# Expert rows added to the outputs by accumulating scatters, the third weight piece fetched during routing, and bias products on four row groups, in a hybrid attention and mixture-of-experts step

## The chip, the cores and the metric

The kernel runs on one core of a Trainium2 chip. The metric is device time in microseconds from start to end of one execution. Engines: TensorE (PE) multiplies matrices and writes PSUM; VectorE (DVE), ScalarE (ACT) and GpSimd (POOL) work element by element; SyncE (SP) issues DMAs. Sixteen DMA engines move data between HBM and SBUF. DMAs that SP or ACT issue go by hardware queues; those that POOL issues, all indirect ones, go by a software queue (q0 in the profile).

## The reference, cut to what matters

One layer for 512 prompt tokens and 8 x 4 sample tokens (544 in all, D = 1024). After three attention-like branches the residual x is complete, and the mixture of experts is added:

```
x = x + mixed @ w_out
logits = h @ router_w + router_b              # h = rmsnorm(x), 32 experts
top, eidx = top_k(logits, 4); gates = softmax(top)
gu   = rows @ w_gu[e] + b_gu[e]               # rows of h, sorted into blocks of one expert
gate = min(gu[:, :1024], 7); up = clip(gu[:, 1024:], -7, 7)
act  = gate * sigmoid(1.702 * gate) * (up + 1)
y    = act @ w_down[e] + b_down[e]
out  = x + sum over the 4 choices of gates * y
```

The outputs that the change touches are y_prompt (512 x 1024) and y_sample (32 x 1024), both float32.

## The kernel before

The program is a row of phases, each an `nc.Block` with one instruction stream per engine and a barrier at its end. Two phases matter here; everything before them (projections, pooling, attention; until about 735 us) is the same in both kernels.

**The routing phase** multiplies the branches by their gates, adds the residual, normalises, computes router logits and sorts the 2176 (token, choice) pairs into blocks of `SLOTS` = 96 rows of one expert. VectorE computes block and slot number of each pair (`blk_f`, `slot_f`), and builds one-hot matrices from them for each tile of 128 tokens (`hot_slot`, `hot_blk`); TensorE multiplies them (L2580) into a table of which token stands in which slot of which block. `spread` (L2587) turns the table so that each partition holds the row numbers that it will gather. `slot_from` is the number of a row's quarter in `scr_h` (normalised x in HBM), `slot_row` that with the choice as well, `slot_gate` the gate. In the same phase the bias b_down is weighted with the gates: `gmat` (token x expert gates) is turned into `gmT` (L2568), and ten products `gmT` x `b_down` (five tiles, two halves of 512) go to PSUM banks (`BD_BANK`); four stand in routing (L2573), six in the next phase (L2888), and VectorE adds all ten to x in the next phase (L2792).

The experts' weights stream through a ring of three slots of 4 MB: two pieces of w_gu, one of w_down, 12 MB a block. The first block's pieces 0 and 1 are issued by SP in the routing phase (L2248, L2253), piece 2 at the start of the next phase (L2662).

**The expert phase** runs a loop over the blocks in use, 32 here. A block's 96 rows are three groups (`G` = 3) of 32 rows, a row cut into four quarters of 256, so that a group is a tile of 128 partitions x 256. Per block:

- POOL copies the index column of block b+1 (L2710) and issues three gathers from `scr_h` into `xg` (L2714); copies gates and target rows of block b (L2729, L2730); for each group waits for ScalarE's scaled result `y_rows` and scatters it into `y_of`, a scratch of 4 x 1024 rows in HBM, one place for each choice of each token (L2735); then it waits until all three scatters have landed (L2739).
- VectorE turns `xg` into `xgT` (L2781) for the next block, and computes the clamped gate between the products.
- TensorE multiplies `xgT` with both w_gu pieces (L2851), then the activation with w_down (L2877), group by group, with the next block's gate bias between (L2861). It waits for `xgT` (e_xT) and for each piece (e_in).
- SP issues each next piece when TensorE has used the slot (L2678).

Indices past the end of the target are dropped (`bounds_check`): that is how padding slots are handled. After the loop SP reads the four rows of each token back from `y_of` (L2687 to L2693), VectorE adds them to x (L2833, L2841), and SP stores the sums as the outputs (L2699, L2702). `x` stays in SBUF throughout.

The order of each engine's instructions is the order in which they are written; nothing is rescheduled.

Of the kernel before, what the change touches and what calls it, by code (L numbers as in the profile page):

```python
# [17 lines left out]
U32 = mybir.dt.uint32  # L18
ALU = mybir.AluOpType
# [194 lines left out]
def build_program(nc, i, o, stop_after=99):  # L214

    ctx = ExitStack()
    with ctx:
# [1898 lines left out]
        slot_row = take(NBLK + 1, GROUPS_E, dt=U32)  # L2116
# [5 lines left out]
        hot_gate = take(NT, TOPK, NE)  # L2122
        assert cursor[0] <= 53000
# [36 lines left out]
        hot_slot = take(2, TOPK, SLOTS)  # L2160
        hot_blk = take(2, TOPK, 2, NBLK + 1)
# [11 lines left out]
        gmT = take(NTOK)  # L2173
# [3 lines left out]
        y_of = scratch("y_of", [TOPK, 1024, D])  # L2177
        hT_at = oT_at - 120 - KD * NTOK
        ring_at = [hT_at, tail_base + KD * D, tail_base]
        end_at = [hT_at, hT_at + 4096, w_gb_at, tail_base + KD * D, tail_base + KD * D + 4096]  # L2180
# [24 lines left out]
        BD_BANK = (1, 2, 3, 4, 5, 6, 7, 0, 1, 2)  # L2205
# [20 lines left out]
        two = lambda ap: ap.rearrange("p (h n) -> p h n", h=2)  # L2226

        with nc.Block() as block:
            @block.sync
            def _(sp):  # L2230
                sp.dma_start(w_up, i["w_up"].rearrange("(k p) n -> p k n", p=128)).then_inc(g_wu, 16)
                for u in range(6, 24):
# [43 lines left out]
            def _(act):  # L2276
# [17 lines left out]
                for n, (cols_n, b) in enumerate(((512, 2), (NTOK - 512, 3))):  # L2294
                    act.wait_ge(r_gmt, n + 1)
                    act.activation(gmT[0:32, 512 * n:512 * n + cols_n], bank(b)[0:32, 0:cols_n], ACT.Copy).then_inc(r_gme, 1)

            @block.vector
            def _(dve):
# [53 lines left out]
                dve.wait_ge(g_rc, 112)  # L2353
# [86 lines left out]
                for n in range(NT):  # L2440
                    r, s = ROWS[n], n % 2
                    if n >= 2:
                        dve.wait_ge(r_hu, n - 1)
                    wide = lambda ap, w: ap.unsqueeze(2).to_broadcast([r, TOPK, w])
                    link(dve.tensor_tensor(hot_blk[0:r, s, :, 1], iota128[0:r, 0:NBLK + 1].unsqueeze(1).to_broadcast([r, TOPK, NBLK + 1]),
                                           wide(blk_f[0:r, n], NBLK + 1), ALU.is_equal))
                    dve.tensor_tensor(hot_slot[0:r, s], iota128[0:r, 0:SLOTS].unsqueeze(1).to_broadcast([r, TOPK, SLOTS]),
                                      wide(slot_f[0:r, n], SLOTS), ALU.is_equal)
                    link(dve.tensor_tensor(hot_blk[0:r, s, :, 0], hot_blk[0:r, s, :, 1], wide(token1[0:r, n], NBLK + 1), ALU.mult))
                    dve.tensor_tensor(hot_blk[0:r, s, :, 1], hot_blk[0:r, s, :, 1], wide(g4[0:r, n], NBLK + 1), ALU.mult  # L2450
                                      ).then_inc(r_hs, 1)
# [4 lines left out]
                dve.wait_ge(r_hu, NT)  # L2456
# [5 lines left out]

                dve.wait_ge(r_sq, 1)
                wide_rows = bank(0)[:, 0:GROUPS_E * 2 * (NBLK + 1)].rearrange("p (g v b) -> p v b g", g=GROUPS_E, v=2)
                dve.tensor_copy(slot_gate, wide_rows[:, 1])
                link(dve.tensor_scalar(slot_row, wide_rows[:, 0], 4.0, cols[:, 4:5], ALU.mult, ALU.add))
                dve.tensor_scalar(slot_from, slot_row, 4095, None, ALU.bitwise_and)

            @block.tensor
            def _(pe):  # L2470
# [21 lines left out]
                pe.wait_ge(g_rc, 112)  # L2492
# [72 lines left out]
                for n in range(NT):  # L2565
                    r = ROWS[n]
                    out = bank(2)[0:32, 128 * n:128 * n + r] if n < 4 else bank(3)[0:32, 0:r]
                    mm = pe.transpose(out, gmat[0:r, n], ident[0:r, 0:r])  # L2568
                    if n >= 3:
                        mm.then_inc(r_gmt, 1)  # L2570
                pe.wait_ge(r_gme, 2)
                for u in range(4):
                    pe.matmul(bank(BD_BANK[u]), gmT[0:32, 128 * (u // 2):128 * (u // 2) + 128],  # L2573
                              b_down[0:32, 512 * (u % 2):512 * (u % 2) + 512], start=True, stop=True).then_inc(p_bd, 1)

                for n in range(NT):
                    r = ROWS[n]
                    pe.wait_ge(r_hs, n + 1)
                    for k in range(TOPK):
                        mm = pe.matmul(bank(7)[0:SLOTS, 128:130 + 2 * NBLK], hot_slot[0:r, n % 2, k],  # L2580
                                       hot_blk[0:r, n % 2, k].rearrange("p v b -> p (v b)"),
                                       start=(n == k == 0), stop=(n == NT - 1 and k == TOPK - 1))
                    mm.then_inc(r_hu, 1)

                pe.wait_ge(r_sp, 1)
                for g in range(GROUPS_E):
                    mm = pe.matmul(bank(0)[:, 2 * (NBLK + 1) * g:2 * (NBLK + 1) * (g + 1)], spread[0:SLOTS, g],  # L2587
# [6 lines left out]
        row_from, row_to = take(4, dt=U32), take(4, dt=U32)  # L2594
# [30 lines left out]
        p_be = sem("p_be")  # L2625
        y_lo = [sem(f"y_lo{n}") for n in range(NT)]
# [316 lines left out]
```

## Time and profile before

| | us |
|---|---|
| median of 3 runs | 1891.73 |
| lowest, highest | 1889.73, 1892.1 |
| span of the profiled execution | 1895.2 |
| TensorE busy | 1738.0 (92%) |
| VectorE busy | 545.6 (29%) |
| ScalarE busy | 335.8 (18%) |
| GpSimd busy | 453.4 (24%) |
| all DMA, mean | 283 GB/s |

The profiled execution is known by its span, from the first instruction to the last; no separate device time is recorded for it. Its span is 3.5 us above the median of the runs. The first 855.7 us of it are everything before the expert blocks, the next 1003 us the 32 blocks, the last 36 us the sums and stores.

### The profile page before, as it was taken

What the parts mean: (1) busy time and instruction counts of PE and PEld (TensorE: products, weight loads), DVE (VectorE), ACT (ScalarE), POOL (GpSimd) and SP (SyncE); (2) the same over time, 40 slices, a digit from 0 to 9 for tenths busy, and PEclk for the clock granted to TensorE, in tenths of its full rate; (3) what the DMA queues carried; (4) which work ended last, traced back from release to release, by engine and by line L of the source; (5) the groups of instructions that cost most, each with busy time, mean ns of one, the idle gap of its engine ahead of it and who ended that gap; (6) DMA issues with size and microseconds to landing.
All of it is one profiled execution on the core that took longest, in us unless ns stands there. A gap on an engine that the chain in (4) does not pass through costs nothing.

```text
span 1895.2 us, 40017 instructions
## 1 busy us (share of the span) xinstructions
PE 1738.0 (92%) x16117; PEld 1000.8 (53%) x16117; DVE 545.6 (29%) x1355; ACT 335.8 (18%) x736; POOL 453.4 (24%) x522
## 2 busy tenths in 40 slices
PE   7997886688899999969999999999999999999992
PEld 3545773344588886533445673555563445443441
DVE  2222014266111111362323131313232323222225
ACT  3232222265200000001111111111111111111110
POOL 1113537376100003311212222222212122222220
PEclk9997977798899999969999999999999999999996
DMA  8207867440421103146999999999999999999986
GB/s 303 100 31 236 301 188 245 160 158 1 178 79 56 56 22 117 45 185 270 416 426 420 422 416 420 420 424 422 415 423 408 422 423 419 423 420 409 426 356 243
DMA packets 84034, 535.54 MB, mean 283 GB/s; under 512 B 19552, under 2 KB 43584, under 8 KB 71009
## 3 DMA queue, kind: packets, MB, share of 16 engines
q1 hardware_dynamic: 62921, 493.44, 64.6%
q0 software_dynamic: 14544, 32.03, 5.0%
q10 hardware_dynamic: 6512, 9.33, 1.5%
q8 instruction: 33, 0.54, 0.1%
q14 instruction: 24, 0.20, 0.0%
HBM read 518.32 MB, written 28.39 MB: 288 GB/s over the span
## 4 chain that ended last, share of the span: by engine, by line
PE 53%; DMA 2%; DVE 0%; SPq 0%; issue 0%; POOLq 0%; POOL 0%; ACT 0%
PE psum L2851 35%; PE psum L2877 18%; DMA arena<-y_of 1%; DMA arena<-scr_h,arena 1%; PE psum L2861 0%; DVE arena L2841 0%; SPq L2689 0%; DMA y_of<-arena 0%; SPq L2687 0%; DVE arena L2781 0%; POOLq L2648 0%; POOL arena L2718 0%; ACT arena L2767 0%; POOLq L2722 0%; POOLq L2718 0%
## 5 line engine op out<-in xcount | busy, mean ns | idle before, releaser
L2851 PE MATMUL psum<-arena 128*32 128x512 f32 x6144 | 668.9, 592 | 3.8 <-DVE arena L2781 2.2
L2851 PEld LDWEIGHTS psum<-arena 128*32 128x32 f32 x6144 | 249.0, 108 | 404.0 <-issue 401.1
L2877 PE MATMUL psum<-arena 128*32 128x256 f32 x6144 | 345.4, 378 | 0.0
L2877 PEld LDWEIGHTS psum<-arena 128*32 128x32 f32 x6144 | 252.0, 109 | 94.0 <-issue 9.8
L2806 DVE TENSOR_TENSOR arena<-psum,arena 128x512 f32<-128x512 f32 x96 | 66.4, 692 | 573.9 <-PE psum L2851 573.9
L2735 POOL DMA_INDIRECT y_of<-arena x96 | 96.9, 1009 | 473.0 <-ACT arena L2767 473.0
L2480 PE MATMUL psum<-arena 128*128 128x272 f32 x768 | 182.9, 396 | 1.8 <-PEq L231 1.8
L2480 PEld LDWEIGHTS psum<-arena 128*128 128x128 f32 x768 | 146.7, 191 | 35.5 <-issue 3.4
L2763 ACT ACTIVATE arena<-arena 128x256 f32<-128x256 f32 x96 | 40.1, 418 | 611.7 <-DVE arena L2808 611.7
L2714 POOL DMA_INDIRECT arena<-scr_h,arena x96 | 99.0, 1031 | 49.3 <-POOL arena L2710 28.5
L799 PE MATMUL psum<-arena 128*128 128x512 f32 (+1 forms) x256 | 90.7, 513 | 0.2 <-DVE arena L660 0.2
L2767 ACT ACTIVATE arena<-psum,arena 128x256 f32<-128x256 f32 x96 | 45.6, 475 | 245.7 <-PE psum L2877 245.7
L2307 DVE TENSOR_TENSOR arena<-psum,arena 128x544 f32<-128x544 f32 x24 | 17.4, 725 | 218.5 <-ACT arena L2282 218.5
L1883 POOL TENSOR_SCALAR arena<-arena 128x512 f32<-128x512 f32 (+3 forms) x64 | 68.5, 1082 | 26.7 <-DVE arena L2010 26.5
L2710 POOL COPY arena<-arena 128x3 uint32 x32 | 6.0, 188 | 279.7 <-DMA y_of<-arena 232.4
L1213 PE MATMUL psum<-arena 128*128 128x256 f32 x256 | 66.0, 415 | 5.5 <-issue 5.5
L2781 DVE STREAM_TRANSPOSE arena<-arena 128x768 f32<-128x768 f32 x33 | 32.2, 977 | 129.5 <-DMA arena<-scr_h,arena 129.5
L422 POOL CAST arena<-arena 32x8 bf16<-32x8 f32 (+1 forms) x6 | 6.2, 1032 | 263.8 <-DMA arena<-in_b_gu 256.9
L799 PEld LDWEIGHTS psum<-arena 128*128 128x128 f32 x256 | 44.1, 191 | 46.9 <-issue 46.6
L444 POOL DMA_INDIRECT arena<-in_cache_slc,arena x60 | 56.9, 949 | 49.0 <-POOLq L231 23.6
L2487 PE MATMUL psum<-arena 128*128 128x272 f32 x256 | 64.3, 399 | 2.3 <-DMA arena<-in_w_up 2.3
L1213 PEld LDWEIGHTS psum<-arena 128*128 128x128 f32 x256 | 52.4, 209 | 15.2 <-issue 5.9
(365 smaller groups left out, 1485.7 us busy)
## 6 DMA issues: line engine op xcount, KB each, us to landing
arena<-in_w_gu SPq DMA_DIRECT2D x64, 4096.0 KB, 15.0
arena<-in_w_down SPq DMA_DIRECT2D x32, 4096.0 KB
arena<-in_w_gb SPq DMA_DIRECT2D x24, 512.0 KB, 3.5
arena<-y_of SPq DMA_DIRECT2D x8, 1024.0 KB, 15.1
arena<-in_cache_cmp SPq DMA_DIRECT2D x62, 128.0 KB, 4.3
arena<-in_cache_slc SPq DMA_DIRECT2D x60, 128.0 KB, 3.0
arena<-in_w_tok SPq DMA_DIRECT2D x3, 2048.0 KB, 12.8
arena<-in_x_all SPq DMA_DIRECT2D x8, 512.0 KB, 11.0
```

The costliest lines, as they stand in the source:

```text
L444: pool.indirect_dma_start(dst, None, i[table], bass.IndirectOffsetOnAxis(page_row[:, at:at + 1], 0)).then_inc(sem, 16)
L799: mm = pe.matmul(bank(2 + c)[0:r, 0:b - a], dstT(n)[:, k], w_tok[:, k, a:b], start=(k == 0), stop=(k == KD - 1))
L1213: mm = pe.matmul(sum_bank(s, c)[:, 0:2 * n].rearrange("p (g b m) -> p g b m", g=2, b=PAGES), w_cmp[:, c, j], turned, start=(j == 0), stop= ...
L1883: ins = pool.tensor_scalar(rows, rows, c[:, g:g + 1], None, ALU.mult)
L2480: pe.matmul(bank(4 * s + h)[:, 0:HALF], w_gb[:, u % 6, k], hT[:, k, t], start=(k == 0), stop=(k == KD - 1))
L2487: mm = pe.matmul(bank(4 * s + 2 + h)[:, 0:HALF], w_up[:, k, 128 * c:128 * c + 128], oT_of(k)[:, t], start=(k == k0), stop=(k == k1 - 1))
L2714: pool.indirect_dma_start(xg[:, g], None, h_quarters, bass.IndirectOffsetOnAxis(row_from[:, g:g + 1], 0), bounds_check=4 * NTOK - 1, oob_i ...
L2735: pool.indirect_dma_start(y_quarters, bass.IndirectOffsetOnAxis(row_to[:, g:g + 1], 0), y_rows[:, g], None, bounds_check=4 * 1024 * TOPK - ...
L2767: act.activation(y_rows[:, g], dn_half(g), ACT.Copy, scale=cur_gate[:, g:g + 1]).then_inc(e_yc, 1)
L2806: dve.tensor_tensor(gu_c[:, g], gu_bank(g), bias_sb, ALU.add).then_inc(e_ba, 1)
L2851: mm = pe.matmul(gu_bank(g)[32 * j:32 * j + 32].rearrange("p (h n) -> p h n", h=2), xgT[:, g, 32 * k:32 * k + 32], gu_w(slot)[:, part, :, ...
L2877: mm = pe.matmul(dn_half(g)[32 * j:32 * j + 32], actT[:, g, 32 * k:32 * k + 32], dn_w(slot)[:, part, 256 * j:256 * j + 256], start=(k == 0 ...
```

## The change

1. The scratch `y_of` and the sums at the end are gone. When the ten bias products are added to x, SP writes x itself to y_prompt and y_sample (five stores, semaphore p_out). POOL waits for them, and then in each block and for each group issues two scatters that add to their target (`compute_op=ALU.add`) instead of one that stores: one into y_prompt by `slot_from`, which drops sample rows, and one into y_sample by `slot_smp` (`slot_from` with the bit of 2048 flipped), which drops prompt rows. POOL waits for all six before it goes on.
2. The third weight piece of block 0 is issued at the end of the routing phase.
3. The bias products: `gmT` and `b_down` stand four times on groups of 32 partitions, so that products of different tiles lie on different row groups of TensorE; order, banks and places are new. Six stand in routing, two of the additions too.
4. The one-hot matrices are built in three batches into buffers of their own instead of two that are reused.

On POOL, in the expert loop, from the gathers of the next block to the loop's end. Before (names: `scr_h` the rows to gather, `y_of` the scratch, `arena` SBUF):

```order
L2714 DMA arena<-scr_h,arena 128x256 x3
L2729 ISA
L2729 COPY arena<-arena 128x3
L2730 ISA
L2730 COPY arena<-arena 128x3
L2731 ISA
L2733 REGISTER_ALU
L2735 DMA y_of<-arena 16384x256
L2733 REGISTER_ALU
L2735 DMA y_of<-arena 16384x256
L2733 REGISTER_ALU
L2735 DMA y_of<-arena 16384x256
```

The same place after the change, from the third copy on:

```order
L2732 COPY arena<-arena 128x3
L2733 REGISTER_ALU
L2735 REGISTER_ALU
L2737 DMA out_y_prompt<-arena 2048x256
L2740 DMA out_y_sample<-arena 128x256
L2735 REGISTER_ALU
L2737 DMA out_y_prompt<-arena 2048x256
L2740 DMA out_y_sample<-arena 128x256
L2735 REGISTER_ALU
L2737 DMA out_y_prompt<-arena 2048x256
L2740 DMA out_y_sample<-arena 128x256
```

One scatter for each group has become two, and a third index copy stands ahead of them.

On TensorE, the end of routing and the start of the expert phase, from the turning of `gmat` to the first block's gate bias. Before:

```order
L2568 MATMUL psum<-arena 32x128 x4
L2568 MATMUL psum<-arena 32x32
L2573 MATMUL psum<-arena 128x512 x4
L2580 MATMUL psum<-arena 96x110 x20
L2587 MATMUL psum<-arena 128x110 x3
```
```order
L2888 MATMUL psum<-arena 128x512 x4
L2888 MATMUL psum<-arena 32x512 x2
L2893 MATMUL psum<-arena 32x512 x4
```

And after, where L2244 is the bias product:

```order
L2593 MATMUL psum<-arena 32x128 x4
L2593 MATMUL psum<-arena 32x32
L2244 MATMUL psum<-arena 128x512 x4
L2606 MATMUL psum<-arena 96x110 x8
L2244 MATMUL psum<-arena 128x512 x2
L2606 MATMUL psum<-arena 96x110 x12
L2616 MATMUL psum<-arena 128x110 x3
```
```order
L2244 MATMUL psum<-arena 128x512 x2
L2244 MATMUL psum<-arena 32x512 x2
L2873 MATMUL psum<-arena 32x512 x4
```

Two bias products moved from the expert phase into routing, between the one-hot products of the first two tiles and the rest.

The diff, cut to its core:

```diff
@@ routing
-        hot_slot = take(2, TOPK, SLOTS)
-        hot_blk = take(2, TOPK, 2, NBLK + 1)
+        hot_slot = take(NT * TOPK, SLOTS)
+        hot_blk = arena[:, w_gb_at:w_gb_at + NT * TOPK * 2 * (NBLK + 1)].rearrange("p (k v b) -> p k v b", v=2, b=NBLK + 1)
-        BD_BANK = (1, 2, 3, 4, 5, 6, 7, 0, 1, 2)
+        BD_UNIT = [(n, h) for h in range(2) for n in range(NT - 1)] + [(NT - 1, 0), (NT - 1, 1)]
+        BD_BANK = (1, 2, 3, 4, 5, 0, 1, 2, 3, 4)
+        BD_EARLY = 6
+        HOT_BATCHES = ((0, 2), (2, 4), (4, NT))
+        def bias_added(dve, u):
+            n, h = BD_UNIT[u]
+            r = ROWS[n]
+            dve.wait_ge(p_bd, u + 1)
+            sl = x[0:r, n, 512 * h:512 * h + 512]
+            dve.tensor_tensor(sl, bank(BD_BANK[u])[0:r], sl, ALU.add).then_inc(p_be, 1)
+        def bias_product(pe, u):
+            n, h = BD_UNIT[u]
+            r, q = ROWS[n], 32 * (n % 4)
+            at = 128 if n == NT - 1 else 0
+            pe.matmul(bank(BD_BANK[u])[0:r], gmT[q:q + 32, at:at + r], b_down[q:q + 32, 512 * h:512 * h + 512],
+                      start=True, stop=True, tile_position=(q, 0)).then_inc(p_bd, 1)
@@ routing, SP
-                                         (b_down[0:32], i["b_down"]),
+                                         *((b_down[32 * q:32 * q + 32], i["b_down"]) for q in range(4)),
+                sp.wait_ge(x_rt, NT)
+                sp.wait_ge(x_lg, NT)
+                sp.wait_ge(r_bp, 12)
                 sp.wait_ge(x_st[0], 48)
                 sp.wait_ge(x_st[1], 32)
+                sp.dma_start(ring[2], weights(slice(0, 1), 2)).then_inc(e_in[2], 16)
@@ routing, VectorE
+                bias_added(dve, 0)
-                dve.wait_ge(r_hu, NT)
+                dve.wait_ge(r_hu, len(HOT_BATCHES))
...
+                bias_added(dve, 1)
                 dve.wait_ge(r_sq, 1)
...
-                dve.tensor_scalar(slot_from, slot_row, 4095, None, ALU.bitwise_and)
+                link(dve.tensor_scalar(slot_from, slot_row, 4095, None, ALU.bitwise_and))
+                dve.tensor_scalar(slot_smp, slot_from, 4 * NP_TOK, None, ALU.bitwise_xor)
@@ expert phase, SP
-                sp.dma_start(ring[2], weights(slice(0, 1), 2)).then_inc(e_in[2], 16)
+                sp.wait_ge(p_be, 2 * NT)
+                for n in range(NT):
+                    sp.dma_start(out_p[128 * n:128 * n + 128] if n < NT - 1 else out_s, x[0:ROWS[n], n]).then_inc(p_out, 16)
...
-                for g in range(G):
-                    sp.wait_ge(e_out[g], blocks * 16)
-                (the ten read-backs from y_of and the six stores)
@@ expert phase, POOL
                 pool.sem_inc(e_sent, 1)
+                pool.wait_ge(p_out, 16 * NT)
...
-                                    pool.indirect_dma_start(y_quarters, bass.IndirectOffsetOnAxis(row_to[:, g:g + 1], 0),
-                                                            y_rows[:, g], None, bounds_check=4 * 1024 * TOPK - 1, oob_is_err=False
-                                                            ).then_inc(e_out[g], 16)
+                                    pool.indirect_dma_start(p_quarters, bass.IndirectOffsetOnAxis(row_to[:, g:g + 1], 0),
+                                                            y_rows[:, g], None, bounds_check=4 * NP_TOK - 1, oob_is_err=False,
+                                                            compute_op=ALU.add).then_inc(e_out[g], 16)
+                                    pool.indirect_dma_start(s_quarters, bass.IndirectOffsetOnAxis(row_smp[:, g:g + 1], 0),
+                                                            y_rows[:, g], None, bounds_check=4 * NS * TS - 1, oob_is_err=False,
+                                                            compute_op=ALU.add).then_inc(e_out[g], 16)
                                 for g in range(G):
-                                    pool.wait_ge(e_out[g], 16 * b + 16)
+                                    pool.wait_ge(e_out[g], 32 * b + 32)
@@ expert phase, VectorE
-                (the sums over the four choices)
```

## Rows read from the trace of the kernel before

**Rows 1.** The page: the span, and the software DMA queue (packets, MB, share).
```profile
span 1895.2 us, 40017 instructions
...
q0 software_dynamic: 14544, 32.03, 5.0%
```

**Rows 2.** The chain that ended last: start us, us, what; one block, then the end.
```profile
1639.75 20.60 PE psum L2851 x192
...
1670.93 20.60 PE psum L2851 x192
...
1860.20 2.36 DMA y_of<-arena
...
1868.47 18.41 DMA arena<-y_of
```

**Rows 3.** Stretches (busy by engine, granted clock, DMA share, GB/s); SP's last weight piece.
```profile
1257.70:1288.90 31.20, 31.20 (x394) 18.16 (x390) 8.59 (x20) 4.43 (x9) 6.61 (x9) 1.00 1.00 420
1840.00:1842.00 2.00, 2.00 (x24) 0.62 (x19) 0.57 (x1) 0.00 (x0) 1.69 (x2) 1.00 0.13 49
...
1827.82 0.33 SPq L2678 DMA_DIRECT2D arena<-in_w_down  x1
```

**Rows 4.** Timeline of POOL and VectorE in that block: start, us, instruction, [idle before <-releaser].
```profile
1634.02 1.04 POOL L2735 DMA_INDIRECT y_of<-arena  x1 [9.82 <-ACT arena L2767]
1641.12 0.98 POOL L2735 DMA_INDIRECT y_of<-arena  x1 [2.43 <-ACT arena L2767]
1650.61 0.19 POOL L2710 COPY arena<-arena 128x3 uint32 x1 [8.50 <-DMA y_of<-arena]
1651.68 1.06 POOL L2714 DMA_INDIRECT arena<-scr_h,arena  x1 [0.89 <-POOL arena L2710]
1654.37 1.04 POOL L2714 DMA_INDIRECT arena<-scr_h,arena  x1 [0.30 <-issue]
1668.35 0.98 DVE L2781 STREAM_TRANSPOSE arena<-arena 128x768 f32<-128x768 f32 x1 [5.33 <-DMA arena<-scr_h,arena]
```

**Rows 5.** Waits from 900 to 1855 us: total, times, longest.
```profile
POOL arena L2710 <- DMA y_of<-arena: 232.4, 27, 9.2
DVE arena L2781 <- DMA arena<-scr_h,arena: 127.6, 30, 5.7
```

**Rows 6.** Timeline around the first block.
```profile
841.32 10.71 PE L2888 MATMUL psum<-arena 32*128 32x512 f32 x12 [2.06 <-PEq L231]
844.74 1.00 POOL L2718 DMA_INDIRECT arena<-scr_h,arena  x1 [0.30 <-issue]
852.07 0.68 DVE L2792 TENSOR_TENSOR arena<-psum,arena 32x512 f32<-32x512 f32 x1 [1.03 <-PE psum L2888]
855.70 1.93 PE L2851 MATMUL psum<-arena 128*32 128x512 f32 x8 [2.19 <-DVE arena L2781]
855.76 0.19 POOL L2710 COPY arena<-arena 128x3 uint32 x1 [10.02 <-DVE arena L2781]
```

**Rows 7.** Timeline in routing.
```profile
822.73 7.19 PE L2573 MATMUL psum<-arena 32*128 32x512 f32 x8 [0.59 <-ACT arena L2296]
829.84 3.17 PE L2580 MATMUL psum<-arena 128*96 128x110 f32 x16
831.66 0.39 DVE L2445 TENSOR_TENSOR arena<-arena 128x220 f32<-128x220 f32 x1 [3.48 <-PE psum L2580]
```

**Rows 8.** DMA issues: count, KB each, median us from issue to landing.
```profile
arena<-in_w_gu SPq DMA_DIRECT2D x64, 4096.0 KB, 15.0
arena<-scr_h,arena POOLq DMA_INDIRECT x99, 10.6
y_of<-arena POOLq DMA_INDIRECT x96, 8.1
arena<-in_cache_slc,arena POOLq DMA_INDIRECT x60, 4.2
arena<-in_cache_cmp,arena POOLq DMA_INDIRECT x48, 5.6
```

More of the change, by code:

```diff
@@ L2122, in build_program @@
         hot_gate = take(NT, TOPK, NE)
+        slot_row = take(NBLK + 1, GROUPS_E, dt=U32)
         assert cursor[0] <= 53000
@@ L2172, in build_program @@
         gmat = take(NT, NE)
-        gmT = take(NTOK)
+        gmT = take(128 + 32)
         b_down = take(D)
@@ L2565, in _ @@
                 for n in range(NT):
[L2566 to L2570, printed above, removed]
+                    r, q = ROWS[n], 32 * (n % 4)
+                    at = 128 if n == NT - 1 else 0
+                    mm = pe.matmul(bank(0)[q:q + 32, at:at + r], gmat[0:r, n], ident[0:r, 0:r], start=True, stop=True,
+                                   tile_position=(0, q))
@@ L2571, in _ @@
+                mm.then_inc(r_gmt, 1)
                 pe.wait_ge(r_gme, 2)
                 for u in range(4):
[L2573 to L2582, printed above, removed]
+                    bias_product(pe, u)
@@ new lines, in _ @@
+                for m, (n0, n1) in enumerate(HOT_BATCHES):
+                    pe.wait_ge(r_hs, m + 1)
+                    for n in range(n0, n1):
+                        r = ROWS[n]
+                        for k in range(TOPK):
+                            nk = TOPK * n + k
+                            mm = pe.matmul(bank(7)[0:SLOTS, 128:130 + 2 * NBLK], hot_slot[0:r, nk],
+                                           hot_blk[0:r, nk].rearrange("p v b -> p (v b)"),
+                                           start=(n == k == 0), stop=(n == NT - 1 and k == TOPK - 1))
@@ L2583, in _ @@
                     mm.then_inc(r_hu, 1)
+                    if m == 0:
+                        for u in range(4, BD_EARLY):
+                            bias_product(pe, u)
                 pe.wait_ge(r_sp, 1)
                 for g in range(GROUPS_E):
-                    mm = pe.matmul(bank(0)[:, 2 * (NBLK + 1) * g:2 * (NBLK + 1) * (g + 1)], spread[0:SLOTS, g],
+                    mm = pe.matmul(bank(6)[:, 128 + 2 * (NBLK + 1) * g:128 + 2 * (NBLK + 1) * (g + 1)], spread[0:SLOTS, g],
                                    slot_pair[0:SLOTS].rearrange("p v b -> p (v b)"), start=True, stop=True)
@@ L2624, in build_program @@
         e_sent = sem("e_sent")
-        p_be = sem("p_be")
-        y_lo = [sem(f"y_lo{n}") for n in range(NT)]
-        y_hi = [sem(f"y_hi{n}") for n in range(NT)]
-        y_half = [sem(f"y_half{h}") for h in range(2)]
-        y_add = sem("y_add")
-        y_done = sem("y_done")
         p_out = sem("p_out")
         USES = PER_BLOCK - 2
-        ORDER = [NT - 1] + list(range(NT - 1))
         GU_K = RING_W // 2048
@@ L2787, in _ @@
                 to_bias_of(0)
-                for u in range(2 * NT):
-                    r = ROWS[u // 2]
-                    dve.wait_ge(p_bd, u + 1)
-                    sl = x[0:r, u // 2, 512 * (u % 2):512 * (u % 2) + 512]
-                    dve.tensor_tensor(sl, bank(BD_BANK[u])[0:r], sl, ALU.add).then_inc(p_be, 1)
+                for u in range(2, 2 * NT):
+                    bias_added(dve, u)
                 to_xgT(0)
@@ L2826, in _ @@
                         dve.nop()
-                link = linked(dve, y_add, [0])
-                for n in ORDER[:-1]:
-                    r = ROWS[n]
-                    for k in range(TOPK):
-                        if k % 2 == 0:
-                            dve.wait_ge((y_lo, y_hi)[k // 2][n], 16)
-                        ins = dve.tensor_tensor(x_end(n)[0:r], x_end(n)[0:r], four(n)[0:r, k], ALU.add)
-                        if k < TOPK - 1:
-                            link(ins)
-                    ins.then_inc(y_done, 1)
-                for h in range(2):
-                    half = slice(512 * h, 512 * h + 512)
-                    dve.wait_ge(y_half[h], 16)
-                    for k in range(TOPK):
-                        ins = dve.tensor_tensor(x_end(ORDER[-1])[:, half], x_end(ORDER[-1])[:, half], four(ORDER[-1])[:, k, half], ALU.add)
-                        if k < TOPK - 1:
-                            link(ins)
-                    ins.then_inc(y_done, 1)
             @block.tensor
@@ L2882, in down @@
                     mm.then_inc(e_y, 1)
-                for u in range(4, 2 * NT):
-                    r = ROWS[u // 2]
-                    if u >= 8:
-                        pe.wait_ge(p_be, u - 7)
-                    pe.matmul(bank(BD_BANK[u])[0:r], gmT[0:32, 128 * (u // 2):128 * (u // 2) + r],
-                              b_down[0:32, 512 * (u % 2):512 * (u % 2) + 512], start=True, stop=True).then_inc(p_bd, 1)
+                for u in range(BD_EARLY, 2 * NT):
+                    pe.wait_ge(p_be, u - BD_EARLY + 1)
+                    bias_product(pe, u)
                 pe.wait_ge(e_bs, 1)
```

77 lines of the change are left out of this document (27 added, 50 removed).

## The prediction

> **What bounds the kernel now.** I began with the page: TensorE is busy for 92% of the span of 1895.2 us [rows 1]. The chain of waits shows that the second half is 32 expert blocks in which TensorE has no gap; one block goes from 1639.75 to 1670.93, 31.2 us [rows 2]. After the last matmul 36 us remain, almost all of it reading back the expert rows (18.4 us), adding and storing [rows 2]. Then the stretches: inside the blocks the DMA share is 1.00 at 420 GB/s, and with all weights fetched it falls to 0.13 [rows 3]. So the DMA engines are as full as TensorE, and whatever is sent besides weights stands in line with them.
>
> The third thing is hidden under TensorE: a chain that runs once round the block. The three scatters of a block are issued from 1634.02 to 1641.12; POOL waits until they have landed before it copies the next rows' indices at 1650.61; three gathers are issued from 1651.68 to 1654.37; VectorE can turn what they bring at 1668.35 and ends at 1669.33; TensorE wants it at 1670.93 [rows 2, 4]. The slack is 1.6 us in this block. VectorE's wait for the gather was 5.33 us here and 127.6/30 = 4.25 us in the mean [rows 4, 5], so the mean slack is 1.6 + 1.1 = 2.7 us. The list of waits shows POOL's side: 232.4 us behind the scatters, 27 times [rows 5].
>
> **The end of the program.** Read-back, sums and final stores go. The last scatter is issued at 1860.20 and, with nothing else in flight, has landed after 2.36 us [rows 2]. Now a second scatter is issued behind it, 1.3 us later (the gathers' spacing, 1651.68 to 1654.37 in two steps [rows 4]), so the span would end at 1860.20 + 1.3 + 2.4 = 1863.9. An accumulating scatter also reads its target, at most another 2.4. I take 1865.2: 30 us saved, bounds 29 and 31.3.
>
> **The start of the blocks.** Today the third weight piece is issued together with the first gathers, the third of them at 844.74, and the products that wait for what they bring begin at 855.70, behind VectorE's turning of it, 1.0 us [rows 4, 6]. With the piece fetched in routing, the gathers meet idle engines: 844.74 + 2.4 = 847.1. The bias additions end next: ten of 0.7 us, paced by six products (12 passes) that take 10.71 us; the last addition ends at 852.75 [rows 6]. Six products now stand before the blocks instead of four; the rest is two large and two small ones (4 x 1.78 = 7.1 us in a row, less if row groups overlap), so additions end at about 848.5, the turning of x and the bias product behind them at about 850. Against 855.70 this saves 5.5 us (bounds 3 and 7).
>
> In routing the four early bias products take 7.19 us from 822.73, and VectorE waits 3.48 us for a one-hot buffer [rows 7]. With all tiles of one-hots in buffers of their own that wait goes: VectorE's ten remaining microseconds of building end near 833. But the products of the first tiles hold PE 3.17 us for two tiles [rows 7], two more bias products (3.6 us in series, 0.9 side by side) come between, and TensorE finishes near 837 to 838.5, where it finishes now. The trace shows no product on row groups, so: worth between -2 and +1.5 us. I take 0, being nearest to the sum of the rows. The larger copy of gmT, three more b_down loads and one VectorE operation (0.25 us) are in that bound. The five output stores (2.2 MB, 5.3 us at 420 GB/s [rows 3]) start at 848.5 and end near 856.5; POOL's next gather waits for them, where today it starts at 855.76 [rows 6]. Against a block that starts 5.5 us earlier it comes 6 us late, once, and block 0 is the one whose gather had most to spare: nothing, with 4 us as the upper bound.
>
> So the fixed part is -30 - 5.5 = -35.5 us.
>
> **Inside the blocks.** This is where the cost is. For each group there are now two scatters, one into the prompt output and one into the sample output; POOL waits for both of all three groups before the next gather. That the second holds few valid rows doesn't make it short: the software queue carried 14544 packets for 99 + 96 + 60 + 48 = 303 DMAs [rows 1, 8], exactly 48 each or three per DMA engine, although a third of the scatters' rows are padding (3072 slots for 2112 rows). So a refused row still has its place in a packet.
>
> What does a packet cost when weights flow? From the first gather's issue to the operand being there it is 1668.35 - 1651.68 = 16.7 us with nine packets per engine; from the third scatter's issue to POOL going on it is 9.5 us with three [rows 4]. The difference gives 1.2 us a packet, plus 5.9 us that don't depend on their number. The packets thus wait in turn behind weight packets; alone, three packets were through in 2.4 us [rows 2].
>
> The Trainium skill (DMA: Bandwidth & Descriptors, "Queues, rings and completion order") says that each engine goes round robin between queues, packet by packet, with some 9 to 17 descriptors in a typical packet. That packets wait in turn agrees with the rows; the three packets per engine and DMA (eight rows and a semaphore write) do not fit its count. Rival B below says what fewer turns would make of the time.
>
> Now 18 packets instead of 9 follow the first scatter's issue, which stands 5.7 us before the block's end E. Served at the loaded price they end at E - 5.7 + 5.9 + 18 x 1.2 = E + 21.8; today POOL goes on at E + 10.9. The rest of the chain (gather, turning) is 18.7 us in this block, 17.6 at the mean slack. If TensorE stalls for s at each block, the chain started at one block's end must fit in s + 31.2 + s, so 2s = L + 17.6 - 31.2, with L the scatters' end behind E. L = 21.8 gives s = 4.1. But a stall also empties the weight queue: pieces are issued when TensorE frees a slot, and the last one, issued at 1827.82, was through some 12.5 us later [rows 3], so the queue idles for s, just while the late scatter packets stand in it. All of them free from E + 12.5 would give L = 14.5 and s = 0.45, too short a pause for that. With a packet costing 0.4 us in the pause (between 0.15 and the 0.8 of 2.36/3), the pause saves 2s: 2s = 21.8 - 2s - 13.6, s = 2.05. With 0.2 us it is 1.2, with 0.8 it is 3.3. For the read of the target I add 0.25 and take 2.3 us a block, for 30 blocks (the first two can't be late by it): +69 us.
>
> The accumulation itself is not in the trace. Lower bound: a plain scatter, nothing. Upper: each accumulating DMA counts as two, a read and a write, so 27 packets, L = 32.6, s = 4.75, +142 us. The valid rows' bytes add only 0.27 MB to the 12.6 MB of a block's weights. I take the value near the low end, since the nearest row, the plain scatter, is priced by turns and not by bytes. The extra index copy (0.2 us on POOL) and the doubled issue (1 us each) are hidden: POOL waits 9.82 us before a block's scatters [rows 4].
>
> Sum: 1895.2 - 35.5 + 69 = 1928.7 us of span. The median of the runs is 3.5 us under this span, so 1925 us.
>
> **Rivals.**
> B, the stall doesn't come: second scatters slip through between weight packets and the 2.7 us of slack carry the rest. Then 1891.7 - 35.5 = 1856 without any stall, up to 1885 with one of 1 us. If the rows of a scatter went in one packet and its semaphore write in another, 12 would follow instead of 18: L = 14.6, s = 0.5, +15 us, 1871. (The Trainium skill's 9 to 17 descriptors in a packet, same section as above, would put a scatter's eight rows per engine into one.) For it speaks that a pause costs little to heal the queue; against it the count of 48 packets for every DMA. The break-even is 35.5/30 = 1.2 us a block.
> C, accumulating rows travel in smaller packets or wait for their read: with one row quarter per packet the prompt scatters have 8 + 1 turns per engine instead of 3, 36 in a block, L = 43.4, 4s = 29.8, s = 7.4, +222 us: 2080. With two read-and-write DMAs' worth it is 1998. The place is POOL's wait at the end of its loop. The Trainium skill (DMA: Bandwidth & Descriptors, "SWDGE vs HWDGE vs iDMA") prefers packets of at most 4096 B; whether bytes read at the target count there no run here shows.
> D, TensorE is not late but weights are: the DMA share is 1.00 already, and 0.6 us of bytes per block would push pieces behind TensorE. A piece lands 15.0 us after issue and is wanted 20.8 later (two thirds of 31.2) [rows 2, 8]: 5.8 us of room, used up after ten blocks, then 0.6 x 20 = 12 us: 1868. Weaker, as it needs the first chain not to bind.
>
> **How the numbers follow.** Forecast (stall of 1.5 to 4.5 us a block, 1900 to 1990): 0.48. B and D: 0.22. A cancelling sum within 0.2% (3.8 us, what a measurement of this kernel can tell): 0.05. C: 0.25. So faster 0.22, same 0.05, slower 0.73. The range for 8 in 10 goes from 1868, into B, to 2050, into C; the forecast's own is 1900 to 1990.
>
> **What would show it.** Right: gaps on TensorE before a block's first products, ended by VectorE's turning of x, uneven from block to block; that turning waiting for the gather, and POOL's copy coming over 12 us after E; 14544 + 96 x 48 = 19152 packets in the software queue; DMA share below 1.00 in the blocks; TensorE's first block at 850; 6 to 8 us between the last matmul and the end. Wrong: gapless TensorE with 31.2 us a block (B); over 30000 packets there (C); gaps ended by weights (D).

## The result and the profile after

| | before | after |
|---|---|---|
| median of 4 runs, us | 1891.9 | 2044.5 |
| span of the profiled execution | 1895.2 | 2032.8 |
| TensorE's first expert block begins | 855.7 | 850.5 |
| last matmul ends | 1858.8 | 2016.3 |
| from there to the end | 36.4 | 16.5 |

The ratio of the times is 1.078 (95% interval 1.074 to 1.083): 7.8% slower. The three terms of the forecast can be read off the two traces: the start came 5.2 us earlier, the 32 blocks took 1165.8 instead of 1003.1 us, and the end 16.5 instead of 36.4. Together -5.2 + 162.7 - 19.9 = +137.6, the difference of the spans. The medians are 153 us apart. The four times of the changed kernel run from 2034.7 (the profiled execution) to 2071.1 us, a slow run that the ratio leaves out.

The page of the changed kernel, to be put beside [rows 1], with the engines' groups:

```profile
span 2032.8 us, 40237 instructions
...
q0 software_dynamic: 37584, 32.15, 7.2%
...
L2834 PE MATMUL psum<-arena 128*32 128x512 f32 x6144 | 689.6, 608 | 142.4 <-DVE arena L2786 139.4
...
L2737 POOL DMA_INDIRECT out_y_prompt<-arena x96 | 152.0, 1584 | 234.9 <-ACT arena L2772 215.4
...
L2740 POOL DMA_INDIRECT out_y_sample<-arena x96 | 150.3, 1566 | 29.3 <-issue 29.0
```

Three things stand here. TensorE waits 142.4 us before the first products of blocks, for VectorE's turning of x (it was 3.8). Those products are also 20.7 us longer in sum than before (689.6 against 668.9); behind the long pauses they run at a low granted clock for a while (stretches below). And the software queue carried 37584 packets where it had 14544: less the 207 gathers at 48 each, that is 27648 for 192 scatters, 144 per scatter or nine per DMA engine. An accumulating scatter puts each of an engine's eight row quarters into a packet of its own, refused rows too. Its issue also takes POOL 1.6 us instead of 1.0.

One round of the chain in the changed kernel (start, us, what), from the last group's second scatter to the next block:

```profile
885.22 1.55 POOL out_y_prompt L2737
887.08 31.50 DMA out_y_sample<-arena
...
923.48 6.84 DMA arena<-scr_h,arena
930.34 0.99 DVE arena L2786
931.45 22.74 PE psum L2834 x192
...
968.48 31.64 DMA out_y_sample<-arena
...
1050.42 10.92 DMA out_y_sample<-arena
...
1114.22 20.11 DMA out_y_sample<-arena
```

In [rows 4] the scatters were done 9.5 us after the last one's issue. Here they take 10.9, 20.1 or 31.5 us, in steps of about the 10.4 us in which TensorE uses up a weight piece. What passes in the 31.5 us from 887.08 can be counted. These are the packets, MB and DMA share of the weights' queue (q1) and of the software queue (q0) from 888 to 894, from 895 to 897 and from 898 to 918 us:

```profile
q1 hardware_dynamic: 76, 2.49, 96.9%
q0 software_dynamic: 75, 0.03, 3.4%
...
q1 hardware_dynamic: 36, 0.72, 89.2%
q0 software_dynamic: 318, 0.01, 10.9%
...
q1 hardware_dynamic: 275, 8.00, 99.4%
q0 software_dynamic: 18, 0.00, 0.1%
```

While weights flow, one software packet goes for each weight packet: 75 beside 76. A 32 KB packet takes 1.21 us (the median of the records), so this is the turn of 1.2 us of the prediction. From 895 to 897 a further 318 pass, where one weight piece has ended and the next begins; TensorE is busy all the while. In the next 20 us only 18 go, about one in the time of one weight packet, and the last 8 pass together at 918. The records don't name the DMA engine, but this is the rate of a single engine that found no such gap until then, and POOL waits for all sixteen.

The waits over the blocks (us, times, longest), beside [rows 5]:

```profile
POOL arena L2710 <- DMA out_y_sample<-arena: 366.1, 26, 41.3
DVE arena L2786 <- DMA arena<-scr_h,arena: 254.4, 24, 29.8
...
PE psum L2834 <- DVE arena L2786: 139.4, 15, 23.0
```

TensorE waits 15 times, about every second block. That is the two-block loop of the forecast: scatters of one block hold up the gather for the block after next. Where TensorE waits, the weight queue drains; the second of these stretches (start:end, then busy us of the engines, granted clock, DMA share, GB/s) is such a pause, the first is all blocks:

```profile
870.00:2016.00 1146.00, 1005.89 (x12252) 422.77 (x12244) 272.22 (x633) 138.34 (x253) 415.98 (x406) 0.94 0.90 353
...
1636.00:1658.00 22.00, 0.15 (x4) 0.00 (x0) 0.20 (x1) 1.32 (x4) 3.76 (x7) 0.56 0.58 239
```

TensorE is idle and the DMA share falls to 0.58. In narrower stretches the granted clock is 1.00 until 1636, 0.50 (the level of 1.2 GHz) from 1640 to 1662, three us into the next products, and 1.00 again from 1664. The products behind such a pause take 22.5 to 23.6 us instead of 20.6.

The start is as it was worked out (timeline, beside [rows 6]). Bias products in 5.62 instead of 10.71 us, the gathers in time, and the first products 5.2 us earlier:

```profile
841.04 5.62 PE L2244 MATMUL psum<-arena 32*128 32x512 f32 x8 [2.34 <-PEq L231]
...
846.70 0.68 DVE L2237 TENSOR_TENSOR arena<-psum,arena 32x512 f32<-32x512 f32 x1 [1.03 <-PE psum L2244]
847.30 0.96 DVE L2786 STREAM_TRANSPOSE arena<-arena 128x768 f32<-128x768 f32 x1
...
850.46 8.11 PE L2834 MATMUL psum<-arena 128*32 128x512 f32 x60 [2.32 <-issue]
```

At the end POOL is alone. The lines of its queue for the last instructions (duration in ns, start in us):

```profile
L2744 POOLq EVENT_SEMAPHORE  x32: 42/43/43, 918.6 to 2023.7; - x32
...
L2680 POOLq COMPARE_BRANCH  x1: 38/38/38, 2028.1 to 2028.1; - x1
L2680 POOLq DRAIN  x1: 4348/4348/4348, 2028.3 to 2028.3; - x1
```

The last scatter has landed at 2023.7. Then POOL runs through the empty passes of its loop until 2028.1 (54 blocks are provided for, 32 used), and waits 4.3 us in the drain that ends the phase. Before, both lay under the read-backs: the last scatter had landed at 1862.6, and the drain began at 1867.2 and took 7.1 us.

### The profile page after: what moved, and what is told of

Read it like the earlier page. It is cut to its first block, busy times and chain, and to the rows that moved or that the text cites. A ratio compares the mean times of both kernels' runs of the same rounds, so it can differ in the third digit from the quotient of the medians.

```text
span 2032.8 us, 40237 instructions
## 1 busy us (share of the span) xinstructions
PE 1749.0 (86%) x16122; PEld 918.0 (45%) x16122; DVE 518.9 (26%) x1324; ACT 334.0 (16%) x736; POOL 664.5 (33%) x650
## 3 DMA queue, kind: packets, MB, share of 16 engines
q0 software_dynamic: 37584, 32.15, 7.2%
## 4 chain that ended last, share of the span: by engine, by line
PE 24%; DMA 22%; issue 7%; POOL 3%; DVE 1%; POOLq 1%; ACT 0%; DVEq 0%
PE psum L2834 20%; DMA out_y_sample<-arena 15%; DMA arena<-scr_h,arena 7%; PE psum L2860 4%; POOL out_y_prompt L2737 1%; POOL out_y_sample L2740 1%; DVE arena L2786 1%; POOL arena L2714 0%; ACT arena L2772 0%; PE psum L2244 0%; POOL arena L2710 0%; POOLq L2725 0%; POOLq L2740 0%; POOLq L2737 0%; POOLq L2714 0%
## 5 line engine op out<-in xcount | busy, mean ns | idle before, releaser
L2834 PE MATMUL psum<-arena 128*32 128x512 f32 x6144 | 689.6, 608 | 142.4 <-DVE arena L2786 139.4
L2834 PEld LDWEIGHTS psum<-arena 128*32 128x32 f32 x6144 | 209.9, 111 | 605.8 <-issue 603.8
L2860 PEld LDWEIGHTS psum<-arena 128*32 128x32 f32 x6144 | 214.7, 109 | 131.3 <-issue 10.8
L2737 POOL DMA_INDIRECT out_y_prompt<-arena x96 | 152.0, 1584 | 234.9 <-ACT arena L2772 215.4
L2505 PEld LDWEIGHTS psum<-arena 128*128 128x128 f32 x768 | 146.0, 190 | 35.0 <-issue 3.4
L2740 POOL DMA_INDIRECT out_y_sample<-arena x96 | 150.3, 1566 | 29.3 <-issue 29.0
L799 PEld LDWEIGHTS psum<-arena 128*128 128x128 f32 x256 | 44.1, 191 | 47.0 <-issue 46.7
```

The source lines that it names most:

```text
L799: mm = pe.matmul(bank(2 + c)[0:r, 0:b - a], dstT(n)[:, k], w_tok[:, k, a:b], start=(k == 0), stop=(k == KD - 1))
L2505: pe.matmul(bank(4 * s + h)[:, 0:HALF], w_gb[:, u % 6, k], hT[:, k, t], start=(k == 0), stop=(k == KD - 1))
L2737: pool.indirect_dma_start(p_quarters, bass.IndirectOffsetOnAxis(row_to[:, g:g + 1], 0), y_rows[:, g], None, bounds_check=4 * NP_TOK - 1, o ...
L2740: pool.indirect_dma_start(s_quarters, bass.IndirectOffsetOnAxis(row_smp[:, g:g + 1], 0), y_rows[:, g], None, bounds_check=4 * NS * TS - 1, ...
L2834: mm = pe.matmul(gu_bank(g)[32 * j:32 * j + 32].rearrange("p (h n) -> p h n", h=2), xgT[:, g, 32 * k:32 * k + 32], gu_w(slot)[:, part, :, ...
L2860: mm = pe.matmul(dn_half(g)[32 * j:32 * j + 32], actT[:, g, 32 * k:32 * k + 32], dn_w(slot)[:, part, 256 * j:256 * j + 256], start=(k == 0 ...
```

## The experiments

All times are medians; the kernel before ran beside them at medians of 1893.6 to 1895.0 us, and ratios are to it. The theories: **T1**, each packet of the software queue waits its turn behind weight packets of 32 KB, and accumulating scatters have three times the packets; **T2**, reading the target makes the accumulation itself slow; **T3**, the doubled issue and wait on POOL are the cost.

### Plain stores

```diff
-                y_rows[:, g], None, ..., oob_is_err=False, compute_op=ALU.add)     # both scatters
+                y_rows[:, g], None, ..., oob_is_err=False)
```

> The changed kernel with both scatters of each group as plain stores (the accumulation is left out, so a token's row holds only its last expert's share). Theory T1 (each packet of the software queue waits its turn behind weight packets, and an accumulating scatter has nine packets per DMA engine instead of three): the queue's packets fall from 37584 to 19152, and the stall in the blocks falls from 4.7 us a block to what the turns' count gives at 27 packets a block, 0 to 2 us: 1880 to 1940 us. Theory T2 (reading the target is what takes the time, not the number of packets): also a fall, to the same numbers, since there is nothing to read. Theory T3 (the doubled issue on POOL and the doubled wait are the cost, accumulating or not): hardly a change, 2000 us or more.

Measured: 1920.2 us, ratio 1.013 (1.010 to 1.015). The page:

```profile
q0 software_dynamic: 19152, 32.09, 5.2%
...
L2832 PE MATMUL psum<-arena 128*32 128x512 f32 x6144 | 682.5, 603 | 55.3 <-DVE arena L2784 52.8
```

19152 packets and 55.3 us of stall, 1.8 us a block. Six scatters instead of three do cost, accumulating or not, but about three fifths of the stall, and 124 of the 153 us, hang on the accumulation. T3 alone is out. T1 and T2 are still both possible.

### One scatter a group

```diff
-                pool.indirect_dma_start(s_quarters, ..., compute_op=ALU.add).then_inc(e_out[g], 16)
...
-                pool.wait_ge(e_out[g], 32 * b + 32)
+                pool.wait_ge(e_out[g], 16 * b + 16)
```

> The changed kernel without the scatters into the sample output (the experts' share of the 32 sample rows is left out), the prompt scatters still accumulating. T1: packets 23760, 36 per engine and block instead of 63; two scatters in three rows' worth of turns go, the stall falls to about 1 us a block or less: 1880 to 1930 us. T2: the sample scatters read almost nothing (4 rows in 66), so nearly the whole stall stays: 1990 us or more, less 8 us at the end for three scatters not issued.

Measured: 1998.2 us, ratio 1.051 (1.044 to 1.059), 23760 packets, and 113.0 us of waits before the blocks. The count is right, but neither theory's time is: too slow for T1 as I had sized it (1 us of stall a block), too near to T2's 1990 to reject it. The 36 packets (27 of them scatters') stall twice as much as the 27 (18) of the plain stores.

### Smaller weight rows

```diff
-                sp.dma_start(ring[slot], weights(bass.ds(e, 1), t)).then_inc(e_in[slot], 16)
+                src = weights(bass.ds(e, 1), t)
+                for j in range(4):
+                    sp.dma_start(ring[slot][:, 2048 * j:2048 * j + 2048], src[:, 2048 * j:2048 * j + 2048]).then_inc(e_in[slot], 16)
```

(and TensorE waits for 64 instead of 16 a piece)

> The changed kernel with each 4 MB weight piece issued as four DMAs of 128 x 8 KB instead of one of 128 x 32 KB; nothing else. T1: a turn then lasts as long as an 8 KB packet, 0.3 instead of 1.2 us, 63 turns fit into a block, and the stall goes: 1880 to 1900 us. T2 and T3: no change, 2030 to 2050 us, as the number of bytes and of scatters is the same. If smaller weight packets cost bandwidth, TensorE would wait for weights instead.

Measured: 1907.6 us, ratio 1.007 (1.005 to 1.009). Accumulation, both scatters, the wait and the number of bytes are untouched, and 137 us of the 153 are gone. This decides between T1 and T2: the cost lies in what the packets wait behind. The time is above the 1880 to 1900 us that T1 was given. The page:

```profile
q0 software_dynamic: 37584, 32.15, 7.4%
...
L2840 PE MATMUL psum<-arena 128*32 128x512 f32 x6144 | 673.4, 592 | 27.6 <-DMA arena<-in_w_gu 24.9
```

As many packets as before, and TensorE no longer waits for the turned x; of the 27.6 us before these products 24.9 are for weights: another wait has taken its place, the last case of the expectation. Four DMAs a piece instead of one is also a change, but the packets show that their length is what counts. From 888 to 894, again six us behind a block's last scatter:

```profile
q1 hardware_dynamic: 334, 2.46, 97.4%
q0 software_dynamic: 334, 0.02, 4.6%
```

Again one for one, but at 0.31 us for a weight packet of 8 KB, and so 334 turns instead of 75 in the same time.

> The changed kernel with each weight piece as two DMAs of 128 x 16 KB. T1: a turn costs 0.6 us, between 1.2 (2044 us) and 0.3 (1907.5 us); of 63 packets per engine and block some 44 find a turn in 31.2 us, so the stall is between the two, 1930 to 1975 us. If only something particular to 32 KB rows were at fault, it would be as with 8 KB: 1905 to 1910 us.

With two DMAs of 128 x 16 KB a piece: 1997.6 us, ratio 1.057 (1.053 to 1.060). In order between 8 KB and 32 KB, but slower than I expected: halving the turn took away 47 us, the next halving 90. The expectation counted the turns of all engines in the mean; the wait is for the last one. An engine that finds no gap between weight pieces needs all its 54 turns: at 0.31, 0.61 and 1.2 us these are 17, 33 and 65 us from a block's first scatter on. That is an estimate, and so is what the chain can bear, 19 us (5.7 to the block's end and 31.2 - 17.6 behind it, by the prediction's terms). Only the 17 us fit. The traces agree: from the last scatter's issue to POOL's next copy it takes 11 to 15 us with 8 KB rows, but 4 to 29 us with 16 KB and 4 to 43 us with 32 KB.

> The kernel before, with each weight piece issued as four DMAs of 128 x 8 KB instead of one of 128 x 32 KB: the control to the run of the changed kernel with 8 KB rows. T1 (a software packet waits one weight packet): the scatters and gathers land sooner (8.1 and 10.6 us median fall below 5), but TensorE waited for neither, so 1888 to 1895 us. If 8 KB rows cost bandwidth with 9 to 31 us of waits of TensorE for weights as in that run: 1900 us or more.

The control, the kernel before with 8 KB rows: 1904.8 us, ratio 1.006 (1.003 to 1.008). Here the other half of the expectation came true. The scatters land after 6.0 us in the median and the gathers after 6.1 (it was 8.1 and 10.6 [rows 8]), and TensorE waits for weights:

```profile
L2883 PE MATMUL psum<-arena 128*32 128x256 f32 x6144 | 344.7, 378 | 7.1 <-DMA arena<-in_w_down 6.6
```

8 KB rows, four DMAs a piece, cost some 10 us by themselves. (In part this is waits too short for the page: the last matmul ended 9.9 us later.)

> The changed kernel with plain stores instead of accumulation (each row holds only its last expert's share) and 8 KB weight rows. Neither a long turn nor extra packets are left. If the 27.6 us that TensorE still waited for weights with accumulation and 8 KB rows are DMA time of the accumulating packets (one row quarter each), they go and what is left is the fixed part of the change: 1892 - 5.2 (start) - 12.7 (end) - 3.4 (six scatters issued in 1.0 instead of 1.6 us each) = 1871 us, 1866 to 1877. If they are the price of 8 KB rows or of six scatters, 1895 us or more.

Measured: 1882.2 us, ratio 0.995 (0.993 to 0.997); TensorE waits 10.4 us for weights, as in the control. Against 1907.6 with accumulation that is 25 us. The time is outside both ranges of the expectation, which had left out the price of the 8 KB rows (10 us); that accounts for the difference to 1871. The 3.4 us at the end did not come: from the last matmul on it is 16.5 us with accumulation and 16.1 without. So the 25 us lie in the blocks, where TensorE waits 16 us longer for weights and the first products take 4.5 us more: the accumulating packets themselves take DMA time, some 20 us.

### The wait moved behind the gathers

```diff
                                 gather(b + 1)
+                                with pool.If(b > 0):
+                                    for g in range(G):
+                                        pool.wait_ge(e_out[g], 32 * b)
+                                with pool.Else():
+                                    pool.nop()
                                 pool.tensor_copy(cur_gate...
...
-                                for g in range(G):
-                                    pool.wait_ge(e_out[g], 32 * b + 32)
```

> The changed kernel, where POOL waits for the scatters of block b-1 not before it issues the gathers of block b+1, but behind them and ahead of the scatters of block b. If the stall is the latency of the chain scatters landed, gather issued, gather landed (T-chain), it goes: 1885 to 1900 us. If it is the throughput of the software queue (63 packets per engine and block, of which some 26 find a turn in 31.2 us, the rest only while no weights flow), the gathers stand behind the scatters' packets in the same queue and nearly the whole stall stays: 2000 to 2045 us.

Measured: 1967.9 us, ratio 1.037 (1.032 to 1.041); 92.2 us of waits before the blocks. Neither: half of the loss goes, half stays. Some 4 us of the gain are at the end (12.3 instead of 16.5 us): POOL waits for the last scatters behind the loop and no longer ahead of its empty passes. In what stays, POOL no longer holds the gathers back, and yet they are late; one of the longest stalls (start, us, what):

```profile
1519.88 0.51 POOL arena L2714
1521.28 1.03 POOL arena L2714
1522.62 36.99 DMA arena<-scr_h,arena
1559.63 0.99 DVE arena L2791
```

The gathers are issued right behind the last scatter of 1517.21 and land 37 us later, behind its packets. The same edit with plain stores tells the two parts apart:

> Plain stores instead of accumulation (each row holds only its last expert's share) and POOL's wait for the scatters behind the next gathers; 32 KB weight rows as in the changed kernel. With plain stores there are 27 packets per engine and block, about as many as find a turn in 31.2 us. If the 55 us of stall with plain stores (1920 us) are the latency of the chain scatters, gather, operand, they go here: 1868 to 1885 us. If they are throughput of the queue, they stay: 1910 to 1920 us.

Measured: 1865.2 us, ratio 0.984 (0.983 to 0.986), 2.8 us below the range expected, and the stall is gone (3.2 of the 55 us are at the end, as above):

```profile
q0 software_dynamic: 19152, 32.09, 5.4%
...
L2837 PE MATMUL psum<-arena 128*32 128x512 f32 x6144 | 667.2, 591 | 4.1 <-issue 3.1
```

With 27 packets per engine and block the stall is the latency of the chain; with 63 it is also the queue's throughput, since the gathers stand behind the scatters' packets wherever POOL waits.

> The changed kernel, accumulating, with 8 KB weight rows and the late wait together. With 8 KB rows (1907.5 us) TensorE waited for weights only, not for the gathered rows. If that is so, the late wait adds nothing: 1903 to 1911 us. If a part of the chain was still felt, it comes out here: 1895 us or less.

Measured: 1905.6 us, ratio 1.005 (1.003 to 1.006), as expected: with 8 KB rows the chain is no longer felt, and 26.2 us of waits for weights remain. The 2 us less come with an end that is 4 us shorter (12.5 instead of 16.5 us).

### The other parts of the change

> The kernel before with the other parts of the change alone: third weight piece in routing, bias products on row groups and reordered, one-hots in batches; scatters into y_of, read-backs and sums as before. The trace of the changed kernel began its first block 5.2 us earlier, so 1894 - 5.2 = 1888.5 us (1885 to 1891), faster than both kernels. If the early start is given back by the first blocks (the gather of block 1 comes no earlier), 1892 to 1895 us.

The kernel before with parts 2 to 4 of the change, and its own scatters and sums: 1887.0 us, ratio 0.9968 (0.9959 to 0.9978). It computes all outputs and is faster than both kernels; of the accumulating kernels that do, none is faster than the kernel before. The two halves by themselves; the first, the bias products alone, is this kernel with the edit:

```diff
-                sp.dma_start(ring[2], weights(slice(0, 1), 2)).then_inc(e_in[2], 16)     # end of routing
...
+                sp.dma_start(ring[2], weights(slice(0, 1), 2)).then_inc(e_in[2], 16)     # start of the expert phase
```

> The kernel before with the bias products on row groups, their order and the one-hot batches, but the third weight piece issued at the start of the expert phase as before. The additions end early (847.4), but the first gathers again share the DMA engines with a 4 MB piece and land at about 854.5: the first block starts at 855.5, as before. 1893.6 us, the same within 1 us. If the bias products were the limit: 1888 us.

> The kernel before with the third weight piece in routing alone. The gathers land at about 847, but the bias additions end at 852.8 as before, then the turning of the operand (1.0 us) and its wake: the first block starts at about 854.3, 1.4 us earlier. 1892 us, within the noise the same. If the piece alone made the whole gain: 1888 us.

Bias products alone: 1893.4 us, ratio 0.9990 (0.9979 to 1.0000). The third piece alone: 1893.4 us, ratio 1.0001 (0.9990 to 1.0011). Neither is worth anything that can be told from no change, together they are worth 6 us. The trace with the bias products alone shows why (timeline):

```profile
846.80 0.68 DVE L2239 TENSOR_TENSOR arena<-psum,arena 32x512 f32<-32x512 f32 x1 [1.03 <-PE psum L2246]
855.88 0.98 DVE L2812 STREAM_TRANSPOSE arena<-arena 128x768 f32<-128x768 f32 x1 [8.40 <-DMA arena<-scr_h,arena]
857.00 1.94 PE L2879 MATMUL psum<-arena 128*32 128x512 f32 x8 [8.75 <-DVE arena L2812]
```

VectorE is through at 847.5 and waits 8.4 us for gathers that share the DMA engines with 4 MB of weights. With the piece alone it is the additions that are late. There VectorE turns x right behind its last addition, with no wait between (all times are 6 us earlier in that profiled run, since the stages before took less):

```profile
845.96 0.68 DVE L2795 TENSOR_TENSOR arena<-psum,arena 32x512 f32<-32x512 f32 x1 [1.03 <-PE psum L2891]
846.57 0.96 DVE L2784 STREAM_TRANSPOSE arena<-arena 128x768 f32<-128x768 f32 x1
```

From the start of the expert phase's bias products to the first block it is 13.8 us with the piece alone, 15.9 with the bias products alone, 8.9 with both and 14.4 before.

## Why the prediction was wrong

The side was right, and so was the mechanism, packets that wait for turns behind weights and a hidden chain that they make too long. The size was not: 33 us of loss were forecast, 153 came, because the packets of an accumulating scatter were taken to be as many as those of a plain one. The time lies near the upper edge of the range, toward rival C (2080), and C's sign came true: 37584 packets in the software queue, where over 30000 were to speak for it and 19152 for the forecast.

- **What bounds the kernel.** Right. DMA engines as full as TensorE, and a hidden chain of scatter, gather and turning with 2.7 us of slack: all that followed happened there.
- **The start, -5.5 us.** Right: -5.2 in the trace, -6 in a kernel of its own. In routing the first four bias products took 2.09 instead of 7.19 us on four row groups, and TensorE ended at 838.7 instead of 839.3: the 0 that I took.
- **The end, -30 us.** Too large: -19.9. The landing was well placed (7.4 us behind the last matmul, 6.4 forecast). Left out was what POOL still has to do once nothing covers it, 4.4 us of empty passes and 4.3 us of drain. The prediction did not ask what the removed read-backs had covered.
- **The price of the turns.** Right in kind and, for the case I sized, in number: 2.05 us a block for 18 scatter packets, and the run with plain stores shows 55.3 us in 30 blocks, 1.8. That the numbers are so near is in part luck: the 0.4 us a packet that gave 2.05 was picked between values that gave 1.2 and 3.3.
- **The step that failed: "For the read of the target I add 0.25 and take 2.3 us a block ... I take the value near the low end".** I argued by bytes where the mechanism counts packets. The accumulating scatters have nine packets per engine instead of three, so 54 follow instead of 18, and the stall is 142.4/30 = 4.7 us a block, plus 0.7 for the longer products behind the pauses. Rival C named just this split, but for the prompt scatters alone, and gave it one chance in four.
- **The formula.** For 54 packets it gives L = 65 and s = 12.9, almost three times what came. It lets packets pass either in turns of 1.2 us or while TensorE stalls. The records show a third way, the gap between two weight pieces: 318 packets from 895 to 897, with TensorE busy. By the rate above it is the last engine that makes the scatters late, not the mean of all.
- **Two smaller slips.** Of the 3072 slots 2176 are filled, not 2112 (544 tokens with four choices each), so 29% of the scatters' rows are padding; nothing in the sum hangs on it. In rival B, L = 14.6 gives s = 0.25 by the formula with the pause, not 0.5, and so 7.5 us instead of 15.
- **Rival D** (weights late) is no cause in the changed kernel, but it is what comes next: with short turns TensorE waits for weights, 24.9 us before the first products.

What stays open: why one DMA engine finds a gap between weight pieces and another doesn't, which makes the stalls so uneven, and how the 25 us between accumulating and plain stores at 8 KB split between the small packets' transfer and the read of the target.

## What to carry to other kernels

When a DMA is hidden behind a saturated stream, price it by its packets times the length of the stream's packet, on the DMA engine that gets no gap, and not by its bytes; count the packets of the operation from the page (queue's packets over DMAs), and where an operation isn't there, expect its packets to differ before its bandwidth does. A shorter packet in the stream helped most here, and its own price had to be measured. When work at the end of a kernel is removed, list what else was running under it: loop exits and drains surface. And of two waits that end at about the same time neither edit shows a gain alone.

## What the runs showed of the hardware that was not expected

- An accumulating indirect scatter of 128 partitions x 1 KB used 144 packets, a plain one 48, whatever share of its rows was refused; POOL took 1.57 to 1.58 us to issue the one and 1.0 us the other.
- A software packet went for each weight packet while both queues had work: 75 beside 76 with 32 KB rows and 334 beside 334 with 8 KB rows, each in six us.
- Bias products with 32 rows of weights on four row groups took 2.09 us for eight passes of 512 columns; on one row group, 7.19 us.
- Issuing each 4 MB piece as 128 x 8 KB rows four times instead of 128 x 32 KB once cost 10 us over 32 blocks, where the DMA share was 0.99 before (416 GB/s) and 1.01 with the short rows (415 GB/s).
- The drain of POOL's queue at the end of the phase took 4.3 us, and 7.1 us in the kernel before.
